# Sums of squares for four RMS norms: slices added on VectorE and GpSimd, fewer ones-products on TensorE, and a new order around the group norms

## The reference

```python
def rms_norm(x, w):
    y = xf * lax.rsqrt(jnp.mean(xf * xf, axis=-1, keepdims=True) + EPS)
    return (y * w.astype(jnp.float32)).astype(x.dtype)
...
    h = rms_norm(x, norm1_w) * (1 + sc1) + sh1             # norm1
...
    y = rms_norm(y.reshape(b, L, SSM_GROUPS, gsz), ssm_norm_w.reshape(SSM_GROUPS, gsz))    # two group norms
    merged = jax.nn.sigmoid(ga) * (o_attn @ w_br_attn) + jax.nn.sigmoid(gs) * (y @ w_br_ssm)
    return merged @ w_out, k, v, new_buf, h_new
...
    x = x + g1 * mix
    h = rms_norm(x, norm2_w) * (1 + sc2) + sh2             # norm2
    x = x + g2 * peer(h, peer_w_query, peer_keys1, peer_keys2, peer_u, peer_v)
...
    y_prompt = rms_norm(xp, norm_f_w)                      # norm_f, for samples too
```

## Time and profile before

| | us |
|---|---|
| median of 3 runs | 4533.72 (4526.81 to 4534.49) |
| the profiled execution, device time | 4537.59 |
| its span, first to last instruction | 4535.9 |
| PE busy | 4253.7 (94%) |
| DVE busy | 3162.1 (70%) |
| ACT busy | 1418.8 (31%) |
| POOL busy | 983.3 (22%) |

### The profile page before, as it was taken

How to read it: one execution, slowest core, us unless ns; L and a number is a source line. 1 busy time by engine, 2 the same in 40 slices (tenths; PEclk the granted TensorE clock), 3 DMA queues, 4 the chain that set the end, 5 groups by cost and what they waited for, 6 DMA issues and landing times. The chain is left out here.

```text
span 4535.9 us, 67898 instructions
## 1 busy us (share of the span) xinstructions
PE 4253.7 (94%) x24256; PEld 2498.9 (55%) x24256; DVE 3162.1 (70%) x5616; ACT 1418.8 (31%) x1943; POOL 983.3 (22%) x1020
## 2 busy tenths in 40 slices
PE   6999997999988899799999999999969999999997
PEld 3665663444455566466555556655635555555554
DVE  4347335455586534555889888988868888988985
ACT  3333421333321112321334444444432222222221
POOL 0000013322200001100142222222234333333320
PEclk8999998999997899999999999999989999999998
DMA  6752766555354677644586777677789888888881
GB/s 226 242 196 102 237 212 213 150 149 151 117 161 134 243 243 261 226 135 139 179 283 246 277 263 286 253 268 275 269 296 339 290 303 288 303 296 289 304 281 40
DMA packets 422568, 1039.54 MB, mean 229 GB/s; under 512 B 38498, under 2 KB 209122, under 8 KB 413730
## 3 DMA queue, kind: packets, MB, share of 16 engines
q0 software_dynamic: 112896, 396.43, 27.1%
q1 hardware_dynamic: 251970, 403.51, 25.7%
q10 hardware_dynamic: 57440, 236.35, 13.7%
HBM read 809.88 MB, written 226.27 MB: 228 GB/s over the span
## 5 line engine op out<-in xcount | busy, mean ns | idle before, releaser
L455 PE MATMUL dot_ps<-h_parts,u_parts 128*128 128x416 f16 x6144 | 1117.0, 340 | 6.8 <-issue 6.8
L455 PE MATMUL totals_ps<-act_parts,v_parts 128*128 128x416 f16 x6144 | 1083.2, 339 | 42.3 <-DVE act_parts L3219 42.3
L455 PEld LDWEIGHTS totals_ps<-act_parts,v_parts 128*128 128x128 f16 x6144 | 601.6, 98 | 522.6 <-issue 44.8
L455 PEld LDWEIGHTS dot_ps<-h_parts,u_parts 128*128 128x128 f16 x6144 | 594.9, 98 | 461.7 <-issue 14.4
L468 PE MATMUL in_ps<-h_parts_in,in_parts 128*128 128x384 f16 (+1 forms) x3168 | 515.6, 319 | 4.5 <-DVE in_parts L826 4.5
L3294 POOL DMA_INDIRECT rows_in<-in_v,row_v x204 | 302.8, 1484 | 497.7 <-DVE h L3238 484.9
L468 PEld LDWEIGHTS in_ps<-h_parts_in,in_parts 128*128 128x128 f16 x3168 | 311.0, 98 | 171.2 <-DVE in_parts L826 4.6
L2572 POOL DMA_INDIRECT u_rows_in<-tmp_u_rows,row_u x192 | 251.0, 1307 | 586.5 <-DVE row_dot L2914 558.3
L3158 ACT ACTIVATE v_parts<-v_group,units 128x1024 f16<-128x1024 f32 x128 | 136.9, 1138 | 766.8 <-PE totals_ps L455 738.1
L2674 ACT ACTIVATE gelu<-dot_ps,units 128x416 f32<-128x416 f32 x256 | 155.6, 608 | 629.4 <-PE dot_ps L455 614.9
L3230 DVE SCALAR_TENSOR_TENSOR h<-totals_ps,sum_unit,h 128x416 f32<-128x416 f32 x388 | 247.9, 647 | 139.9 <-PE totals_ps L455 139.3
(11 more groups left out here) (402 smaller groups left out, 5899.4 us busy)
## 6 DMA issues: line engine op xcount, KB each, us to landing
u_chunks<-in_u SPq DMA_DIRECT2D x128, 512.0 KB, 6.2
v_group<-in_v SPq DMA_DIRECT2D x31, 2048.0 KB, 8.3
tmp_g<-gelu ACTq DMA_DIRECT2D x128, 416.0 KB, 5.3
tmp_w<-h ACTq DMA_DIRECT2D x26, 2048.0 KB, 10.3
w_groups<-tmp_w SPq DMA_DIRECT2D x32, 1664.0 KB, 11.6
gelu_in<-tmp_g SPq DMA_DIRECT2D x31, 1664.0 KB, 7.5
tmp_u_rows<-proj_rows ACTq DMA_DIRECT2D x64, 512.0 KB, 5.4
attend_v_sweep<-in_v ACTq DMA_DIRECT2D x64, 512.0 KB, 4.3
```

The source lines that it names most:

```text
L455: mm = pe.matmul(bank, left(x), right(y), start=first and x == 0 and y == 0, stop=last and x == 1)
```

## The change

Five things change.

1. `Norm`: VectorE adds the squared slices into slice 0 (`add`, one TENSOR_TENSOR of 128x1088 for each further slice, each waiting for the one before), and TensorE then does three ones-products in place of three for each slice. This holds for norm1, both group norms and norm2.
2. `merge_phase`, start: TensorE does the `wa` products of output slice 0 ahead of the ones-products of the group norms. Both groups share PSUM banks 3 to 5, so that group 1's ones-products also wait until group 0's sums are read.
3. `norm2`: ScalarE squares a slice inside the w_out loop, one step after it is complete, and VectorE adds it one step later still, right behind `add_gated` and ahead of the query sweep. The w_out loops of VectorE and ScalarE are written out.
4. `sums_phase`, last group: the four transposes come right behind the third and fourth output slice; `gated` runs for each slice as soon as it is drained, on 832 columns, and a new `gated_rows` does the other 256 columns of all slices after slice 4.
5. `norm_f` moves into `sums_phase`: ScalarE squares, GpSimd adds slices 1 to 4 into slice 0, and TensorE does ones-products for that sum and for slices 5, 6 and 7 (12 in place of 24).

```diff
+    def add(self, dve, k):
+        dve.wait_ge(self.squared, k + 1)
+        if k > 1:
+            dve.wait_ge(self.added, k - 1)
+        total = self.sq[:, 0, :]
+        dve.tensor_tensor(total, total, self.sq[:, k, :], ALU.add).then_inc(self.added, 1)
+
     def tensor(self, pe):
         ones = self.s["const"][:, C_ONE:C_ONE + P]
-        for k in range(self.chunks):
-            pe.wait_ge(self.squared, k + 1)
-            for i, (t0, n) in enumerate(SPLITS):
-                mm = pe.matmul(self.psum[:, i, 0:n], ones, self.sq[:, k, t0:t0 + n],
-                               start=(k == 0), stop=(k == self.chunks - 1))
-                if k == self.chunks - 1:
-                    mm.then_inc(self.summed, 1)
+        pe.wait_ge(self.added, self.chunks - 1)
+        for i, (t0, n) in enumerate(SPLITS):
+            pe.matmul(self.psum[:, i, 0:n], ones, self.sq[:, 0, t0:t0 + n], start=True,
+                      stop=True).then_inc(self.summed, 1)
...
@@ merge_phase, tensor
-                group[0].tensor(pe)
-                group[1].tensor(pe)
+                def branch(i, u, norms=False):
+                    pe.wait_ge(br_in[u], (i + 1) * 64)
+                    for j, (t0, n) in enumerate(SPLITS):
+
+                        pe.wait_ge(banks_taken, i * (2 * NS) + u * NS + j + 1)
+                        for k in range(NA):
+                            pe.matmul(ps[:, j, 0:n], wa[:, u, k, :], o[:, k, t0:t0 + n],
+                                      start=(k == 0), stop=(k == NA - 1))
+                        if not norms or j < 2:
+                            turn_fill(i * 2 + u, j)
+                    if norms:
+                        group[0].tensor(pe)
+                        pe.wait_ge(group[0].meaned, NS)
+                        group[1].tensor(pe)
+                        turn_fill(0, 2)
+                    if u == 0:
+                        pe.wait_ge(y_ready, KC)
...
                 pe.wait_ge(o_in, 16)
+                branch(0, 0, True)
+                branch(0, 1)
+                with pe.Fori(1, KC // 2) as i:
...
@@ merge_phase, scalar
+                for m in range(KC):
+                    for at in range(PASS * Turned.FILLS):
+                        to_rows.scalar(act, KC + m, PASS, at // Turned.FILLS, at % Turned.FILLS, SWEPT)
+                        if m > 0 and at == 4:
+                            act.wait_ge(mix_taken, m + 2)
+                            norm.square(act, m - 1)
                 act.wait_ge(mix_taken, KC + 2)
-                norm.scalar(act)
+                norm.square(act, KC - 1)
+                norm.roots(act)
@@ merge_phase, vector
+                    add_gated(dve, link, x[:, m, :], gate, src, ps[:, u * NS + NS - 1, SEQ - t0:n],
+                              spare[:, u, :, :]).then_inc(mix_taken, 1)
+                    if m > 1:
+                        norm.add(dve, m - 1)
+                    for k in range(Q_PASS):
+                        query_sweep.vector(dve, m, Q_PASS, k, NK)
+                norm.add(dve, KC - 1)
+                norm.means(dve)
...
@@ sums_phase, tensor
-                        if isinstance(g, int) and g == LAST and 2 <= m < 2 + BACKS:
-                            back(m - 2)
+                            if isinstance(g, int) and g == LAST and m in (2, 3):
+                                back(m * ND - 4 + q)
@@ sums_phase, vector
                         if g == LAST:
-                            for k in GATED_AT.get(m, ()):
-                                gated(k)
+                            gated(m)
+                            if m == ROWS_GATED:
+                                gated_rows()
...
+                def gated_rows():
+
+                    dve.wait_ge(back_taken, BACKS)
...
+                    link.mark(dve.tensor_tensor(own, own, gate, ALU.mult))
+                    for k in range(KC):
+                        to = acc[:, k, TD:SEQ]
+                        dve.scalar_tensor_tensor(to, to, s["mod"][:, 5 * KC + k, 0:1], x_of(k)[:, TD:SEQ],
+                                                 ALU.mult, ALU.add)
+                    link.wait(link.base + link.n)
+                    for k in range(KC):
+                        to = acc[:, k, SEQ:T]
+                        ins = dve.tensor_tensor(to, to, x_of(k)[:, SEQ:T], ALU.add)
+                    ins.then_inc(rows_gated, 1)
@@ sums_phase, gpsimd
+                total = square_of(0)
+                for k in range(1, BY_POOL + 1):
+                    pool.wait_ge(norm.squared, k + 1)
+                    if k > 1:
+                        pool.wait_ge(norm.added, k - 1)
+                    pool.tensor_tensor(total, total, square_of(k), ALU.add).then_inc(norm.added, 1)
@@ sums_phase, scalar
+                for k in range(KC):
+                    if k < ROWS_GATED:
+                        act.wait_ge(rows_gated, 1)
+                    act.wait_ge(dense_gated, k + 1)
+                    if 2 < k < KC - 1:
+                        act.wait_ge(norm.added, k - 2)
+                    act.activation(square_of(k), acc[:, k, :], ACT.Square).then_inc(norm.squared, 1)
+                norm.roots(act)
```

More of the change, by code:

```diff
@@ L228, in __init__ @@
         self.squared = sem(name + "_squared")
+        self.added = sem(name + "_added")
         self.summed = sem(name + "_summed")
@@ L2096, in _ @@
+                        branch(i, u)
                 pe.wait_ge(br_taken, KC * NS)
@@ L2112, in _ @@
             def _(act):
+                to_rows.begin(act)
                 group[0].squares(act)
@@ L3115, in _ @@
                 rounds(sp, turn)
+                for k in range(KC):
+                    sp.wait_ge(y_ready, k + 1)
+                    sp.dma_start(a["y_out"][:, k, :], acc[:, k, :]).then_inc(y_out, 16)
+                sp.wait_ge(y_out, 16 * KC)
             @block.tensor
@@ L3148, in total @@
                             mm.then_inc(sum_done, 1)
-                        if isinstance(g, int) and g == LAST and 2 <= m < 2 + BACKS:
-                            back(m - 2)
+                            if isinstance(g, int) and g == LAST and m in (2, 3):
+                                back(m * ND - 4 + q)
                 pe.sem_inc(sum_done, PER)
                 rounds(pe, total, 1)
+                pe.wait_ge(back_taken, BACKS)
+                pe.wait_ge(held_taken, NS)
+                ones = s["const"][:, C_ONE:C_ONE + P]
+                for k in (0, *range(BY_POOL + 1, KC)):
+                    if k == 0:
+                        pe.wait_ge(norm.added, BY_POOL)
+                    else:
+                        pe.wait_ge(norm.squared, k + 1)
+                    for i, (t0, n) in enumerate(SPLITS):
+                        mm = pe.matmul(norm.psum[:, i, 0:n], ones, square_of(k)[:, t0:t0 + n], start=(k == 0),
+                                       stop=(k == KC - 1))
+                        if k == KC - 1:
+                            mm.then_inc(norm.summed, 1)
             @block.scalar
@@ L3287, in _ @@
                     turn(g, g % 2, g // 2)
+                norm.means(dve)
+                for k in range(KC):
+                    x = acc[:, k, :]
+                    dve.scalar_tensor_tensor(x, x, s["par"][:, W_NF + k:W_NF + k + 1], s["rstd"][:, :], ALU.mult,
+                                             ALU.mult).then_inc(y_ready, 1)
             @block.gpsimd
```

119 lines of the change are left out of this document (44 added, 75 removed).

## The result

The changed kernel takes 4558.31 us in the median of 5 runs (4553.36 to 4563.71), the kernel before beside it 4533.72 (4526.81 to 4539.18): the ratio is 1.0051, with a 95% interval of 1.004 to 1.0063. It is slower, by 0.5%. The changed kernel's profiled execution has a span of 4555.6 us, 19.7 more than that of before.

A forecast was written before the change was run, and what follows sets the result against it. TensorE, busy 94% of the span, was taken as the bound, with VectorE's chain setting the pace around norms. Terms summed to +10.2: 4547.8 against the profiled 4537.6, or 4544 for the median; range 4534 to 4555.

The forecast's parts named there:

- Merge's start: Start of merge: `wa` products wait for loads ahead of the ones-products, so the first `y` product comes later; costs 25.9 us.
- The w_out loop: w_out loop: adds ahead of the query sweep delay expert loads by 0.9 us in five steps; costs 4 us.
- norm2's tail: From the last `add_gated` to norm2's first reciprocal: early squares and three products; gains 9.1 us.
- The end: End of the program: earlier gating, GpSimd's four adds and twelve products before norm_f's reciprocals; gains 10 us.
- norm1: norm1: seven adds and three slow products end sooner, half given back by slow conditioning products; gains 0.6 us.
- the first (the delay is given back): Rival: the branch loop gives back its late start; sum -15.7 without the 25.9, so 4518 us; chance 0.06.
- The third (the loop doesn't notice the adds): Rival: w_out loads are held by the transfer queue; +6.2, 4540 us; chance 0.18, shared with cheap GpSimd adds.
- The second: Rival: GpSimd's adds at the end are dear or held up, 3.9 each; total +15.3, 4549 us; chance 0.16.

The follow-up runs named there:

- e1: Changed kernel, but the group norms' ones-products stand ahead of the `wa` products again, in banks of their own; VectorE's adds stay: 4535.92 us, ratio 1.0.
- e8b: Kernel before, with both query loads of a w_out step behind its four expert loads in GpSimd's queue: 4530.86 us, ratio 0.9988.
- r_before: Kernel before, unedited, run once more for a second profile: one run, 4540.12 us.
- e5b: Changed kernel with merge's start as before: both group norms' squares multiplied slice by slice by TensorE, ahead of the `wa` products: 4527.21 us, ratio 0.9983.
- e7b: Changed kernel with e5b's start of merge, e2's and e4's order in the w_out loop and e6's end: 4505.38 us, ratio 0.9938.
- e12: Changed kernel, but ScalarE's first write of expert rows per w_out step waits until GpSimd has issued its second expert load: 4545.94 us, ratio 1.0029.
- e4: Changed kernel, but both query loads of a w_out step stand behind its four expert loads in GpSimd's queue: 4544.05 us, ratio 1.0018.
- e2: Changed kernel, but each norm2 add in the w_out loop stands behind the two query sweeps: 4541.71 us, ratio 1.0019.
- e6: Changed kernel, but each `norm_f` square has its own buffer and TensorE multiplies slices 5 to 7 first, GpSimd's sum last: 4544.65 us, ratio 1.002.
- e9: Changed kernel, with norm2's adds behind the query sweeps and idle VectorE adds of growing size ahead of the sweeps: one run, 4550.06 us.
- e11: Changed kernel, but ScalarE's first write of expert rows per w_out step waits until GpSimd has issued its first expert load: 4552.4 us, ratio 1.0038.
- e10: Changed kernel, with one idle ScalarE instruction just ahead of its first write of expert rows in each w_out step: 4553.49 us, ratio 1.0043.

## Why the prediction was wrong

It had the sign and the place of each term, and it missed the size: +10.2 by its sum, +18.2 by the stretches, and a median of 4558.31 outside the range of 4534 to 4555.

- **Merge's start, +25.9: right.** It measured +25.5 (the working gave 26.3, and 0.4 were taken off by judgement). The traces stand 4.0 us apart here (the first squaring of `y` is at 1497.06 in place of 1501.1). With that taken off, the first `wa` product was forecast at 1514.9 and came at 1514.63, group 1's first mean at 1545.8 (came at 1545.15), the first `y` product at 1560.8 (came at 1560.10). One part was off by 1.2 us: the ones-products were forecast at 1526.0 and came at 1524.78, as the clock was at full (2.4 GHz) from about 1518.4, 3.8 us after the first product and not 5. What the term left out is what comes after it: the branch loop took 1.6 us more. Its clock stood at half (1.2 GHz) for some 6 us from the first `y` product on, where in both profiles of the kernel before it did for some 3. The window of the changed kernel, in the columns of the earlier trace rows:

```profile
1560.00:1566.00 6.00, 5.90 (x11) 3.37 (x12) 2.30 (x3) 0.00 (x0) 0.53 (x1) 0.50 0.29 87
```

  In all sixteen profiles the branch loop's time goes with this stretch at half clock: 198.4 to 198.8 us where it lasted 2.9 to 3.7 us, 199.8 where it lasted 5.5 (e1), 199.9 to 200.1 where it lasted 5.9 to 6.2. That the change causes the longer one is not shown. e8b has the start of the kernel before, with a pause of 4.05 us ahead of the first `y` product as in r_before, and still 6.2 us at half clock; e5b and e7b have a pause of 9.7 us and only 3.4 and 3.5.

- **The w_out loop, +4: wrong, +7.8.** This is the step that failed most. The delay of 0.9 us per step was right (0.87 measured), and so were its parts: the way from `add_gated` to VectorE's next work took 1.84 us without the register instructions (forecast 1.85), and the add 1.20. What failed is the price of a late load. It was taken to be its lateness alone, and a load that is issued later by 0.87 us took 1.2 us more to land, because ScalarE's write is now issued ahead of it. The sum had no term for that. e12 put the write behind the load again, with GpSimd's issues as in the changed kernel: the loop cost 1.9 us. So about 5.9 of the 7.8 us are the write's, which I had at nothing, and 1.9 are the delay's own, which I had at 4: TensorE's waits grew by 2.4 us for five delays of 0.87, so the steps had more slack than I gave them. The gain of the register instructions is real only inside this chain: with the loads early, the loop of before takes 147.7 us (e8b) and the written-out one 147.3 (e4).
- **norm2's tail, -9.1: right,** -9.0. The three products took 4.00 us where 3.7 were expected.
- **The end, -10: -7.7.** The mechanism was right. The first add started 0.35 us later than forecast; the four adds took 11.55 us with their gaps in place of 10.6; TensorE and the last mean took 1.1 us more, mostly because its clock stayed at half longer than the 3 us that I gave it (0.50 from 4524.0 to 4529.0):

```profile
4524.00:4529.00 5.00, 4.88 (x8) 2.87 (x9) 0.00 (x0) 3.39 (x3) 0.00 (x0) 0.50 0.00 0
```

  An add takes 2.47 to 2.50 us when no gating starts ahead of it, below my 2.6; two of the four take 3.08, with VectorE's gating in their way, and the gatings take 2.27 and 1.77 in place of 1.08.
- **norm1, -0.6: about 0.** The stretch up to the first input product was 83.4 and 83.0 us before and 82.3 to 85.1 in the kernels with the change. The norm itself is as forecast: from VectorE's copy to the last ones-product it takes 14.3 us, where it took 14.8. The conditioning products behind it then take 14.2 and 14.7 us in place of 13.9, for they start at half clock, and give that back.
- **The rest.** Of the miss of 8.0, w_out makes 3.8, the end 2.3, the branch loop 1.6 and norm1 0.6; merge's start takes 0.4 off. The mended sum, 4533.7 + 18.2 = 4551.9, is inside the range. The first measurement lies 6.4 us above that and the second, by its ratio, 2.2. Where those 2 to 6 us lie is open: the stretches outside the table were 1.5 us longer in the changed kernel in the first pair of profiles, and 10.0 us shorter in the second.

Of the rivals, the first (the delay is given back) fell by e1 and e5b. The third (the loop doesn't notice the adds) fell by e2 and e4. The second had GpSimd's adds at 3.9, too dear, but part of its mechanism is there: they are held up by VectorE. The Trainium skill's "SBUF — State Buffer", section "SBUF: two separate sides", says that such a pair of instructions locks each other out, and the trace agrees nearly in full (last section). The estimate by that rule, a gain of 7 at the end, is nearer to the 7.7 than my 10, though two gatings stood between the adds and not three. The Trainium skill's "GPSIMD Engine Reference", section "Elementwise — side-by-side cycle accounting", gave an estimate of 2.39 for an add alone, 3% below the 2.47 measured.

## What to carry to other kernels

Before an instruction is put ahead of another in a queue, look at what its own semaphores wait for: twelve products that had been free in a shadow cost 19 us when they were moved ahead of the chain that made the shadow, since their load was under way. A delay in a chain of loads can cost more than its length if it carries an issue past that of another queue; so check the distance to the neighbours' issues, not only the slack, and order a queue by when each load is needed. Fewer products bought nothing at merge's start: the adds that replace them lie on VectorE's chain, and the few products left run at half clock (6.2 us in e1). What did help at the end was buffers that let engines run past each other (7.9 us in e6). How much of norm2's 9.0 and of the end's 7.7 is early squaring and how much fewer products, no run took apart.

## What the runs showed of the hardware

- The first of GpSimd's two expert loads of 512 KB was in use 5.4 to 5.9 us after its issue where ScalarE's write of the same size was issued 0.49 us or more behind it (nine steps of e9 and e12), and 6.6 to 7.2 us where the write was issued at most 0.21 us behind it, or up to 0.36 ahead (sixteen steps of e9, e11 and two traces of the changed kernel). At +0.44 us, in the two traces of the kernel before, it took 5.8 to 6.2 in the steps where TensorE waited for it, and once 7.8. At -0.66 it took 6.1 and 6.3. The Trainium skill's "DMA: Bandwidth & Descriptors", section "Queues, rings and completion order", has each engine take turns between the queues by packets. That would share the time, and the traces agree so far: the write's own landing shows where the time goes. It landed 4.0 to 4.5 us after its issue where it was 0.35 us ahead, 5.3 to 5.6 at 0.07 ahead or behind, 6.7 at +0.21, and 6.7 to 7.6 from +0.42 to +0.64. What the load gains the write loses, and only the load is waited for by TensorE. Why it is a jump within 0.3 us, no run shows. Nor does the distance alone decide: in e8b, with another order in GpSimd's queue, the same load landed 6.0 to 7.0 us after its issue in six of seven steps with the write 0.49 us behind it.
- GpSimd's add and VectorE's gating exclude each other nearly in full. In e6 the gating that began at 4507.51 ended at 4509.79, 0.88 us after the first add's end at 4508.91 (a gating alone takes 1.08); the second add began at 4509.06 and took 3.10 us, 0.63 more than alone, of the 0.73 in which the gating still ran. VectorE's drains of PSUM, with one SBUF input, kept their 0.65 us beside the same adds.
- ScalarE issues a DMA while an activation ahead of it still runs (0.14 us after its start, in e10). That idle instruction did not delay it; a semaphore did (e11, e12).
- Three stretches that no edit touched vary. That of the `z` products took 506.0 to 506.5 us in six profiles and 501.5 to 502.5 in the other ten. It was the same both times for the two kernels that were profiled twice, and went with TensorE's wait for the load of `in_cache_k`: 13.4 us in the kernel before, 10.4 in the changed one. Between the last `dot_ps` product and the first of `totals_ps` it took 41.8 to 45.4 us, and the `dot_ps` products 1192.4 to 1199.9. What decides these is open; it is why one profile's span can't be set against one other's for a change of a few us.
